# Two-layer hybrid decoder on eight cores: the last norm's gain and bias in one block on GpSimd, x loads and residual scaling moved into v_B and u

## The chip, the cores and the metric

The kernel runs on the 8 cores of one Trainium2 chip. Each core works alone on 8192 of the 65536 tokens (two sequences of 4096), with no communication between cores. The metric is the device time of the slowest core in microseconds (us). A core has TensorE for matmuls (PE in the profile; its weight loads are PEld), VectorE (DVE), ScalarE (ACT), GpSimd (POOL) and SyncE (SP), which issues DMAs here. Each engine works off its own instructions strictly in the order in which they were written; engines wait for each other through semaphores.

## The reference, cut to what matters

```python
x = _layernorm(x, ln_in_g, ln_in_b)
for l in range(2):
    h = x @ w_in[l] + b_in[l]
    q, k, v, g_a, u_b, v_b, g_b, r_a, r_b = _split_cols(h)
    y_a = _swa_sinks(q, k, v, sinks[l]) * silu(g_a)      # window 128, 8 query heads, 2 kv heads
    y_b = _chunked_sgu(gelu(u_b), gelu(v_b), ...) * silu(g_b)   # norm of v, 128x128 mixing per chunk
    merged = sigmoid(r_a) * (y_a @ p_a[l]) + sigmoid(r_b) * (y_b @ p_b[l])
    out = merged @ w_out[l] + b_out[l]
    x = _layernorm(ALPHA * x + out, ln_g[l], ln_b[l])
```

x is (16, 4096, 1024) in float32, D_MODEL is 1024, q, g_a, u_b, v_b and g_b are 512 columns wide, r_a and r_b 1024.

## The kernel before

**Tiles and stages.** Tokens go in tiles of 512 (four blocks j of 128 tokens). A stage is one tile in one layer; a core has 32 stages, numbered 0 to 31, ordered (tile 0, layer 0), (tile 1, layer 0), (tile 0, layer 1), (tile 1, layer 1), then tiles 2 and 3, and so on. So stages 4n and 4n+1 are layer 0 of a new pair of tiles, stages 4n+2 and 4n+3 are layer 1. **Kind 0, 1, 2 or 3** below is the stage number modulo 4. Stages 0 and 1, and 2 and 3, share some work; from stage 4 on all stages run the same loop.

**One stage of the loop, in PE's order.** First `out`: the output projection of the stage before, four blocks of 2x8 matmuls, reading the eight merged tiles `tRb` 0 to 7. Its first matmul is called the stage's *opening* here. Then `vb`, `u`, `gb`, `ga`: the projections v_B, u, gate_B, gate_A, four tiles of eight matmuls each; in `ga` each tile is followed by a spatial-gating step whose result VectorE turns into `mixed` and then into `gbT`. Then attention with the 16 tiles r of the two route projections: scores (`kpad,qT` in PE's rows) alternate with r tiles. Then `pb` (8 tiles, with transposes of the next stage's input), `q` of the next stage (4 tiles), `pa` (8 tiles) and `kv` of the next stage. In `pa` VectorE makes two instructions for each tile: `tRa<-tRa,ps` (from PSUM), then `tRb<-tRa,tRb`, an add whose inputs both lie in SBUF. The eighth add makes the last tile that `out` needs, in its eighth matmul.

**PSUM.** `q`, `kv`, `out`, `vb`, `u`, `gb`, `ga`, `pb` and `pa` rotate through five banks; r tiles have three and scores three. PE waits when the bank it needs has not been read out by ScalarE or VectorE.

**What sets the order.** The code is written region by region; *hooks* put extra steps behind a named tile: `("out", 2)` is behind block 2 of `out`, `("vb", 1)` behind the second v_B tile. A step joins each engine's queue there and is carried out when the queue comes to it, which may be long before PE reaches the named tile.

**The norm behind `out`.** VectorE adds the residual and takes statistics. After blocks 1 and 3 a variance goes to GpSimd, which raises it to the power -0.5 (`sm_p<-sm_p,neghalf`, `ln_rstd`); then VectorE forms the bias (`ln_bias`, L269 `sm_p<-mv_p,sm_p`) and ScalarE applies both (`second`, and `to_bf` when a layer follows). The gain and bias rows of the norm are applied by GpSimd two stages later in `third_hooks`: for each block four instructions `xres<-xres,gb` on 128x512 float32 (`ln_gb`), 16 in all, called *pieces* here. After layer 1 the block is then stored as y by SP. In kinds 0 and 1 the same buffer next takes the tile's new x (`load` in `resid_hooks`), which ScalarE scales (`app`, `xres<-xres,sm_i`) and GpSimd gives the input norm's gain and bias (again `ln_gb`, 16 pieces) as the residual.

**The input norm** of a new tile goes through `stg`: powers `sm_i` on GpSimd at ("q", 1) of kinds 2 and 3 and at ("vb", 1) of kinds 3 and 0; `lnin_hooks` puts the applications of blocks 2 and 3 (`xbf<-stg,sm_i`) behind u tiles.

**Weights** stream through four ring slots. SP loads them as bf16 from an internal buffer; at first use of each slab GpSimd issues the load from the float32 original (`ring<-wpk`), which happens up to stage 6.

Of the kernel before, what the change touches and what calls it, by code (L numbers as in the profile page):

```python
# [152 lines left out]
def build(n_tok, seq_len):  # L153
# [24 lines left out]
    def sb(name, shape, dt=F32):  # L178
        return es.enter_context(nc.sbuf_tensor(name, list(shape), dt))
# [24 lines left out]
    gb = sb("gb", [128, 6, D])  # L204
# [73 lines left out]
    def dma(eng, out, in_, reads, writes, chan, batch=False):  # L278
        P.add(eng, lambda e: e.dma_start(out=out, in_=in_), reads, writes, chan=chan, batch=batch)
# [86 lines left out]
    stages = []  # L366
# [108 lines left out]
    def ln_apply(k, j, out, okey, src, skey):  # L475
        j0 = j & ~1
        act(out, src, AF.Identity, (skey, ("sm1", k, j0), ("sm2", k, j0)), (okey,),
            bias=sm[k][:, 2, j:j + 1], scale=sm[k][:, 1, j:j + 1])

    def ln_gb(buf, j, gi, eng="pool"):  # L480
        key = ("xres", buf, j)
        for h in range(2):
            c = slice(h * 512, (h + 1) * 512)
            d = xres[:, buf, j, c]
            tt(eng, d, d, gb[:, gi, c], ALU.mult, (key, ("gb", gi)), (key,))
            tt(eng, d, d, gb[:, gi + 1, c], ALU.add, (key, ("gb", gi + 1)), (key,))
# [102 lines left out]
        for i, (k, f) in enumerate(zip(at[1:], (to_bf, second, to_bf, second))):  # L589
            hook(hooks, k, (lambda f, j: lambda: f(j))(f, 2 + i // 2))  # L590

    def third_hooks(s, hooks, at=(("out", 0), ("out", 1), ("out", 2), ("out", 3)),
                    to=(("vb", 0), ("vb", 1), ("vb", 2), ("u", 0))):

        t, l = stages[s]
        buf, gi = t % 2, 2 * (l + 1)

        def out_dma(j):
            r0 = t * 512 + j * 128
            dma("sp", y_d[r0:r0 + 128, :], xres[:, buf, j, :], (("xres", buf, j),), (("y", t, j),), ("yo", buf, j))  # L600
# [72 lines left out]
    def hook(hooks, k, f):  # L673
        hooks.setdefault(k, []).append(f)
# [38 lines left out]
    def lnin_hooks(s, hooks, at=(("vb", 1), ("u", 2), ("u", 3))):  # L713
        load, stats, apply = lnin_parts(s)
        hook(hooks, at[0], lambda: stats(2))
        hook(hooks, at[1], lambda: apply(2))
        hook(hooks, at[2], lambda: apply(3))

    def resid_hooks(s, hooks):
        t, l = stages[s]  # L720
        buf, k = t % 2, "i%d" % (t % 2)

        def load(j):
            r0 = t * 512 + j * 128
            dma("sp", xres[:, buf, j, :], x_d[r0:r0 + 128, :], (), (("xres", buf, j),), ("xr", buf, j))

        def app(j):
            d, key = xres[:, buf, j, :], ("xres", buf, j)
            ln_apply(k, j, d, key, d, key)

        if s < 2:
            at = (("r", 15), ("pb", 1), ("pb", 3), ("pb", 5))
        else:
            at = (("gb", 1), ("gb", 3), ("ga", 1), ("pb", 1))
        for j in range(4):
            if s > 1:
# [267 lines left out]
    for s in range(NS):  # L1004
        hooks = {}
# [23 lines left out]
        if s > 1:  # L1029
            third_hooks(s - 2, hooks, *THIRD.get(s, ()))  # L1030
        if s == NS - 1:
            third_hooks(s - 1, hooks, (("gb", 0), ("gb", 2), ("ga", 0), ("ga", 2)),
                        (("ga", 0), ("ga", 2), ("r", 0), ("r", 2)))
        if s == 3:
            lnin_hooks(s, hooks, (("r", 2), ("r", 6), ("r", 10)))
        elif s > 0 and is_lnin(s):
            lnin_hooks(s, hooks)
        if is_lnin(s + 1):
            lnin_before(s + 1, hooks)
        if stages[s][1] == 0:  # L1040
            resid_hooks(s, hooks)
# [94 lines left out]
```

How the kernel before makes its waits and increments, by code:

```python
        def run(ename, e):  # L100
            seen = {}
            for op in per_eng[ename]:
                waits = {}
                for d in op.deps:
                    if d.chan is None and d.eng == "pe" and ename == "pe" and op.chan is None:
                        continue
                    s, v = event(d)
                    if v > waits.get(s, (None, 0))[1]:
                        waits[s] = (s, v)
                if op.chan is not None and not self.chan_batch[op.chan] and op.ticket > 1:
                    s = csem[op.chan]
                    v = 16 * (op.ticket - 1)
                    if v > waits.get(s, (None, 0))[1]:
                        waits[s] = (s, v)
                for s, v in waits.values():
                    if seen.get(s, 0) < v:
                        e.wait_ge(s, v)
                        seen[s] = v
                ins = op.fn(e)
                if op.chan is not None:
                    ins.then_inc(csem[op.chan], 16)
                elif op.signal:
                    ins.then_inc(esem[ename], 1)
            if ename == "sp":
                for c, s in csem.items():
                    v = 16 * self.chan_count[c]
                    if seen.get(s, 0) < v:
                        e.wait_ge(s, v)
                        seen[s] = v
```

## Time and profile before

| | us |
|---|---|
| median of 3 runs | 3554.02 (3551.52 to 3555.46) |
| profiled execution | 3556.13 |
| its slowest core (core 2), span | 3554.5 |
| the other cores, span | 3531.3 to 3548.6 |
| PE busy | 3400.5 (96%) |
| DVE, ACT, POOL busy | 2316.1, 1814.9, 1396.1 |
| granted TensorE clock, core 2 | 0.989 |

All rows are of core 2. Times in the trace are counted from the start of the span. A matmul of 512 columns is shown with 0.38 us, but eight in a row take 1.89 us, so one starts every (1.89 - 0.38) / 7 = 0.216 us. In brackets behind a row stands how long the engine sat idle before it and what ended the wait. An instruction on VectorE or GpSimd that is itself held up shows as a longer one, not as idle time. Openings named below: stage 12 at 1383.00, stage 13 at 1493.22, stage 14 at 1600.28, stage 15 at 1706.70, stage 16 at 1812.29.

### The profile page before, as it was taken

How to read it: one execution, taken by the hardware profiler on the slowest of the kernel's cores; microseconds unless marked ns; L12 is line 12 of the kernel's file. 1: busy time of each engine (PE TensorE's matmuls, PEld its weight loads, DVE VectorE, ACT ScalarE, POOL GpSimd, SP SyncE). 2: the span in 40 equal slices, each digit the busy share in tenths (PEclk: the TensorE clock that was granted, in tenths of full speed). 3: DMA queues.
4: the chain of work that ended last, by engine and by line, in shares of the span. 5: the costliest groups of instructions: out<-in, count | busy, mean ns of one | idle time of the engine just before them, and what ended most of it. 6: DMA issues, size and time to landing. Idle time of an engine off the chain costs nothing.

```text
span 3554.5 us, 61689 instructions; the slowest of 8 cores (3531.3 to 3554.5 us)
## 1 busy us (share of the span) xinstructions
PE 3400.5 (96%) x18320; PEld 1596.8 (45%) x18320; DVE 2316.1 (65%) x4993; ACT 1814.9 (51%) x4059; POOL 1396.1 (39%) x1284
## 2 busy tenths in 40 slices
PE   5999889989999999999999999999999999999997
PEld 2444334434444444444444444444444444444443
DVE  3675665646766666766676666666667667666667
ACT  4455345635456445465445465455555554555543
POOL 1343243533245333452344432444134533255343
PEclk9999999999999999999999999999999999999999
DMA  9666875564444445354454444553445534455342
GB/s 183 157 163 115 223 177 184 172 178 160 160 165 171 163 149 186 136 174 146 168 194 152 147 147 161 197 184 130 149 149 190 184 137 156 154 170 192 137 137 108
DMA packets 97095, 577.77 MB, mean 163 GB/s; under 512 B 11010, under 2 KB 11266, under 8 KB 41348
## 3 DMA queue, kind: packets, MB, share of 16 engines
q1 hardware_dynamic: 90580, 535.08, 43.2%
q0 software_dynamic: 5472, 38.28, 6.9%
q8 instruction: 159, 2.61, 0.3%
q14 instruction: 164, 1.34, 0.1%
q10 hardware_dynamic: 720, 0.46, 0.1%
HBM read 550.18 MB, written 61.87 MB: 172 GB/s over the span
## 4 chain that ended last, share of the span: by engine, by line
PE 91%; DVE 3%; issue 2%; DMA 2%; ACT 2%; POOL 1%; DVEq 0%; SPq 0%; ACTq 0%; POOLq 0%
PE ps L248 88%; PE ps L495 2%; PE ps L894 2%; DMA ring<-wpk 1%; DVE gbT L259 1%; POOL xres L259 1%; DVE tRa L269 0%; DVE sm_i L269 0%; ACT xT L256 0%; ACT Pq L868 0%; ACT L868 0%; DVE nmx L861 0%; DMA xres<-x 0%; DVE ps L858 0%; DVE xres L269 0%
## 5 line engine op out<-in xcount | busy, mean ns | idle before, releaser
L248 PE MATMUL ps<-xT,ring 128*128 128x512 bf16 x8080 | 1875.1, 381 | 36.5 <-DMA ring<-wpk 30.0
L248 PEld LDWEIGHTS ps<-xT,ring 128*128 128x128 bf16 x8080 | 782.9, 98 | 965.5 <-issue 83.7
L259 POOL TENSOR_TENSOR xres<-xres,gb 128x512 f32<-128x512 f32 x762 | 987.5, 1300 | 206.9 <-ACT xres L256 124.5
L259 POOL TENSOR_TENSOR Pq<-Pq,rcp 128x512 bf16<-128x512 bf16 x256 | 261.4, 1042 | 1030.2 <-DVE rcp L881 836.3
L868 ACT ACTIVATE Pq<-ps,nmx 128x128 bf16<-128x128 f32 x1024 | 370.8, 374 | 314.1 <-DVE nmx L269 311.6
L248 PE MATMUL ps<-ring,tRb 128*128 128x512 bf16 x2016 | 443.6, 380 | 12.0 <-DMA ring<-wpk 9.7
L248 PEld LDWEIGHTS ps<-ring,tRb 128*128 128x128 bf16 x2016 | 196.3, 98 | 245.2 <-issue 20.0
L256 ACT ACTIVATE xres<-xres,sm_p 128x1024 f32<-128x1024 f32 (+1 forms) x129 | 155.6, 1218 | 273.5 <-DVE sm_p L269 270.5
L248 PE MATMUL ps<-ring,xT 128*128 128x128 bf16 (+1 forms) x1920 | 286.9, 300 | 0.0
L259 POOL TENSOR_TENSOR sm_p<-sm_p,neghalf 128x2 f32<-128x2 f32 (+1 forms) x66 | 45.7, 692 | 552.9 <-DVE sm_p L263 543.4
L248 PE MATMUL ps<-gbT,ring 128*128 128x512 bf16 x1024 | 256.0, 379 | 0.0
L861 DVE TENSOR_REDUCE nmx<-ps 128x2 f32<-128x256 f32 x512 | 217.5, 425 | 55.3 <-DVE ps L858 3.2
L269 DVE SCALAR_TENSOR_TENSOR tRa<-tRa,ps 128x512 bf16<-128x512 bf16 x256 | 174.1, 680 | 121.4 <-PE ps L248 121.2
L269 DVE SCALAR_TENSOR_TENSOR xres<-xres,ps 128x512 f32<-128x512 f32 x256 | 174.9, 683 | 89.6 <-PE ps L248 84.9
L248 PE MATMUL ps<-gaT,ring 128*128 128x512 bf16 x992 | 221.0, 379 | 6.5 <-DVE tRa L269 5.0
L248 PE MATMUL ps<-kpad,qT 128*128 128x512 bf16 x512 | 195.4, 382 | 32.5 <-DVE nmx L861 17.9
L256 ACT ACTIVATE xT<-ps,cs 128x512 bf16<-128x512 bf16 x256 | 185.7, 780 | 75.2 <-PE ps L495 75.1
L858 DVE COPY_PREDICATED ps<-upper,ps 128x256 f32<-128x256 uint16 x496 | 208.0, 419 | 12.2 <-PE ps L248 12.0
L868 ACT ACTIVATION_READ_ACCUMULATOR Pq<-ps,nmx 128x1 f32 x1024 | 214.9, 210 | 0.0
L259 DVE TENSOR_TENSOR uT<-uT,gbT 128x512 bf16<-128x512 bf16 x120 | 79.5, 673 | 202.5 <-ACT gbT L256 202.5
L256 ACT ACTIVATE xbf<-xres,sm_p 128x1024 bf16<-128x1024 f32 x64 | 79.1, 1236 | 251.3 <-DVE sm_p L269 251.3
L248 PEld LDWEIGHTS ps<-ring,xT 128*128 128x128 bf16 x1920 | 150.5, 98 | 121.5 <-issue 2.4
(117 smaller groups left out, 3773.2 us busy)
## 6 DMA issues: line engine op xcount, KB each, us to landing
ring<-ws SPq DMA_DIRECT2D x368, 1024.0 KB, 5.0
xres<-x SPq DMA_DIRECT2D x64, 512.0 KB, 8.1
y<-xres SPq DMA_DIRECT2D x60, 512.0 KB, 5.3
ring<-wpk POOLq DMA_DIRECT2D x29, 1024.0 KB, 13.5
stg<-x SPq DMA_DIRECT2D x56, 512.0 KB, 5.6
ws<-ring SPq DMA_DIRECT2D x25, 1024.0 KB, 10.8
ring<-ws SPq DMA_DIRECT2D x28, 512.0 KB, 3.7
gb<-gbr SPq DMA_DIRECT2D x6, 512.0 KB, 12.3
```

Of the source, the lines that this page charges most:

```text
L248: P.add("pe", lambda e: e.matmul(out, lhsT, rhs, start=start, stop=stop), reads, writes)
L256: P.add("act", lambda e: e.activation(out=out, in_=in_, func=func, **kw), reads, writes)
L259: P.add(eng, lambda e: e.tensor_tensor(out=out, in0=in0, in1=in1, op=op), reads, writes)
L269: P.add("dve", lambda e: e.scalar_tensor_tensor(out=out, in0=in0, scalar=s, in1=in1, op0=op0, op1=op1), reads, writes)
L495: P.add("pe", (lambda o, i: lambda e: e.transpose(out=o, in_=i, identity=ident_bf[:]))(o, i), (("xbf", j), ("ident",)), (("ps", BX),))
L858: P.add("dve", lambda e: e.copy_predicated(out=o[:, :, 1, :], mask=upper[:].bitcast(mybir.dt.uint16).rearrange("p (h k) -> p h k", h=2), d ...
L861: P.add("dve", lambda e: e.tensor_reduce(out=nmx[:, q, 2 * c:2 * c + 2], in_=o[:, :, 1, :], axis=mybir.AxisListType.X, op=ALU.max, negate= ...
L868: P.add("act", (lambda hk: lambda e: e.activation(out=Pq[:, q, hk * 4 + c, :], in_=o[:, hk, 1, :], func=AF.Exp, scale=0.125, bias=nmx[:, q ...
L894: P.add("pe", (lambda h: lambda e: e.transpose(out=psP[:, h * 128:(h + 1) * 128], in_=Pq[:, q, h, :], identity=ident_bf[:]))(h), (("Pq", q ...
```

## The change

```diff
-    def third_hooks(s, hooks, at=(("out", 0), ("out", 1), ("out", 2), ("out", 3)),
-                    to=(("vb", 0), ("vb", 1), ("vb", 2), ("u", 0))):
+    def third_hooks(s, hooks, at=(("out", 0),) * 4, to=(("out", 0), ("out", 1), ("out", 2), ("out", 3))):
...
         if s < 2:
             at = (("r", 15), ("pb", 1), ("pb", 3), ("pb", 5))
+        elif s % 2 == 0:
+            at = (("vb", 1), ("vb", 3), ("u", 1), ("u", 3))
         else:
-            at = (("gb", 1), ("gb", 3), ("ga", 1), ("pb", 1))
+            at = (("vb", 1), ("u", 0), ("u", 1), ("gb", 1))
         for j in range(4):
             if s > 1:
-                hook(hooks, (("u", 1), ("u", 2), ("u", 3), ("gb", 0))[j], (lambda j: lambda: load(j))(j))
+                hook(hooks, (("out", 3), ("vb", 0), ("vb", 1), ("vb", 2))[j], (lambda j: lambda: load(j))(j))
...
         elif s > 0 and is_lnin(s):
-            lnin_hooks(s, hooks)
+            if stages[s][1] == 0:
+                lnin_hooks(s, hooks, (("vb", 1), ("gb", 2), ("ga", 0)))
+            else:
+                lnin_hooks(s, hooks)
```

No instruction is added or removed. The default places of `third_hooks` are used from stage 4 on; stages 2 and 3, and the extra call in stage 31, name their own places and keep them. `resid_hooks` acts in kinds 0 and 1, the new `lnin_hooks` places in kind 0.

GpSimd's queue in a stage of kind 0, from the power at ("q", 1) of the stage before (`sm_i`) to the attention's scaling of probabilities (`Pq`). `sm_p` are the powers of the norm behind `out`, `sm_v` those of v_B, `xres` the pieces. Before:

```order
L259 TENSOR_TENSOR sm_i<-sm_i,neghalf 128x2
L273 COPY kpad<-kpad 128x2x128
L273 COPY vbuf<-vbuf 128x128
L259 TENSOR_TENSOR xres<-xres,gb 128x512 x4
L259 TENSOR_TENSOR sm_p<-sm_p,neghalf 128x2
L259 TENSOR_TENSOR xres<-xres,gb 128x512 x8
L259 TENSOR_TENSOR sm_p<-sm_p,neghalf 128x2
L259 TENSOR_TENSOR xres<-xres,gb 128x512 x4
L259 TENSOR_TENSOR sm_v<-sm_v,neghalf 128x2
L259 TENSOR_TENSOR sm_i<-sm_i,neghalf 128x2
L259 TENSOR_TENSOR sm_v<-sm_v,neghalf 128x2
L259 TENSOR_TENSOR xres<-xres,gb 128x512 x12
```

The same place in the changed kernel:

```order
L259 TENSOR_TENSOR sm_i<-sm_i,neghalf 128x2
L273 COPY kpad<-kpad 128x2x128
L273 COPY vbuf<-vbuf 128x128
L259 TENSOR_TENSOR xres<-xres,gb 128x512 x16
L259 TENSOR_TENSOR sm_p<-sm_p,neghalf 128x2 x2
L259 TENSOR_TENSOR sm_v<-sm_v,neghalf 128x2
L259 TENSOR_TENSOR sm_i<-sm_i,neghalf 128x2
L259 TENSOR_TENSOR xres<-xres,gb 128x512 x4
L259 TENSOR_TENSOR sm_v<-sm_v,neghalf 128x2
L259 TENSOR_TENSOR xres<-xres,gb 128x512 x12
```

The 16 pieces of the last norm stand together ahead of both `sm_p` powers, and the first four pieces of the residual stand between the two `sm_v` powers.

ScalarE's queue in a stage of kind 1, from the read-out of the v_B tiles (`vbg`) to the first gate_A tiles (`gaT`). `xres<-xres,sm_i` is the residual's scaling. Before:

```order
L256 ACTIVATE vbg<-ps 128x512 x4
L256 ACTIVATE xbf<-xres,sm_p 128x1024
L256 ACTIVATE uT<-ps,cs 128x512
L256 ACTIVATE xres<-xres,sm_p 128x1024
L256 ACTIVATE uT<-ps,cs 128x512 x2
L256 ACTIVATE xbf<-xres,sm_p 128x1024
L256 ACTIVATE uT<-ps,cs 128x512
L256 ACTIVATE gbT<-ps,cs 128x512
L256 ACTIVATE xres<-xres,sm_p 128x1024
L256 ACTIVATE gbT<-ps,cs 128x512
L256 ACTIVATE xres<-xres,sm_i 128x1024
L256 ACTIVATE gbT<-ps,cs 128x512 x2
```

In the changed kernel, over the middle of the same stretch:

```order
L256 ACTIVATE xres<-xres,sm_i 128x1024
L256 ACTIVATE xres<-xres,sm_p 128x1024
L256 ACTIVATE uT<-ps,cs 128x512
L256 ACTIVATE xres<-xres,sm_i 128x1024
L256 ACTIVATE uT<-ps,cs 128x512
L256 ACTIVATE xbf<-xres,sm_p 128x1024
L256 ACTIVATE uT<-ps,cs 128x512
L256 ACTIVATE gbT<-ps,cs 128x512
L256 ACTIVATE xres<-xres,sm_p 128x1024
L256 ACTIVATE gbT<-ps,cs 128x512
L256 ACTIVATE xres<-xres,sm_i 128x1024
L256 ACTIVATE gbT<-ps,cs 128x512 x2
```

Before, one of the four scalings stood ahead of the last two `gbT` read-outs; now all four do (the first, behind two of the `vbg` read-outs, is above the rows shown).

GpSimd's queue at the opening of stage 4, with the weight loads that GpSimd issues. Before:

```order
L273 COPY vbuf<-vbuf 128x128
L279 DMA ring<-wpk 128x4096
L259 TENSOR_TENSOR xres<-xres,gb 128x512 x4
L259 TENSOR_TENSOR sm_p<-sm_p,neghalf 128x2
L259 TENSOR_TENSOR xres<-xres,gb 128x512 x8
L259 TENSOR_TENSOR sm_p<-sm_p,neghalf 128x2
L259 TENSOR_TENSOR xres<-xres,gb 128x512 x4
L279 DMA ring<-wpk 128x4096 x2
```

In the changed kernel:

```order
L273 COPY vbuf<-vbuf 128x128
L279 DMA ring<-wpk 128x4096
L259 TENSOR_TENSOR xres<-xres,gb 128x512 x16
L259 TENSOR_TENSOR sm_p<-sm_p,neghalf 128x2 x2
L279 DMA ring<-wpk 128x4096 x2
```

Both powers now stand between the pieces and the two loads, of which the first fetches the gate_B slab.

## Rows read from the trace of the kernel before

**Rows 1.** The page, part 4: the chain that ended last, by engine

```profile
PE 91%; DVE 3%; issue 2%; DMA 2%; ACT 2%; POOL 1%; DVEq 0%; SPq 0%; ACTq 0%; POOLq 0%
```

**Rows 2.** Windows, stages 12 to 14: us; busy PE, PEld, DVE, ACT, POOL; clock; DMA

```profile
1383.00:1493.22 110.22, 106.85 (x575) 50.09 (x573) 73.85 (x158) 56.83 (x127) 53.92 (x47) 0.98 0.51 179
1493.22:1600.28 107.06, 105.36 (x576) 49.75 (x573) 71.64 (x147) 58.87 (x129) 53.02 (x46) 1.00 0.50 171
1600.28:1706.70 106.42, 105.48 (x576) 49.58 (x574) 70.43 (x153) 57.06 (x127) 32.34 (x31) 1.00 0.40 143
```

**Rows 3.** Timeline of PE, fourth scores of stages 12 and 13: start, us, what

```profile
1435.43 0.59 PE L248 MATMUL ps<-kpad,qT 128*128 128x512 bf16 x1 [3.24 <-DVE nmx L861]
...
1543.85 0.38 PE L248 MATMUL ps<-kpad,qT 128*128 128x512 bf16 x1 [1.44 <-ACT Pq L868]
```

**Rows 4.** Timeline of DVE, last gbT products of stages 12, 13, 14

```profile
1429.28 2.57 DVE L259 TENSOR_TENSOR gbT<-mixed,uT 128x512 bf16<-128x512 f32 x2
...
1537.77 2.51 DVE L259 TENSOR_TENSOR gbT<-mixed,uT 128x512 bf16<-128x512 f32 x2
...
1644.41 1.28 DVE L259 TENSOR_TENSOR gbT<-mixed,uT 128x512 bf16<-128x512 f32 x2
```

**Rows 5.** Timeline of POOL, stage 12

```profile
1372.00 5.50 POOL L259 TENSOR_TENSOR xres<-xres,gb 128x512 f32<-128x512 f32 x4
1392.99 0.70 POOL L259 TENSOR_TENSOR sm_p<-sm_p,neghalf 128x2 f32<-128x2 f32 x1 [15.49 <-DVE sm_p L263]
...
1421.94 17.89 POOL L259 TENSOR_TENSOR xres<-xres,gb 128x512 f32<-128x512 f32 x12 [9.19 <-ACT xres L256]
```

**Rows 6.** Timeline of DVE, `pa` ahead of stage 12's opening

```profile
1373.51 1.45 DVE L259 TENSOR_TENSOR tRb<-tRa,tRb 128x512 bf16<-128x512 bf16 x1
1374.88 0.67 DVE L269 SCALAR_TENSOR_TENSOR tRa<-tRa,ps 128x512 bf16<-128x512 bf16 x1
1375.66 0.71 DVE L259 TENSOR_TENSOR tRb<-tRa,tRb 128x512 bf16<-128x512 bf16 x1
...
1378.22 0.42 DVE L259 TENSOR_TENSOR tRb<-tRa,tRb 128x512 bf16<-128x512 bf16 x1
...
1383.85 0.42 DVE L259 TENSOR_TENSOR tRb<-tRa,tRb 128x512 bf16<-128x512 bf16 x1
```

**Rows 7.** Timeline of PE, kv tile and opening of stage 12

```profile
1379.49 1.89 PE L248 MATMUL ps<-xT,ring 128*128 128x512 bf16 x8 [0.21 <-DVE tRa L269]
...
1383.00 4.26 PE L248 MATMUL ps<-ring,tRb 128*128 128x512 bf16 x19
```

**Rows 8.** Timelines of POOL and DVE, `pa` ahead of stage 13's opening

```profile
1478.10 5.49 POOL L259 TENSOR_TENSOR xres<-xres,gb 128x512 f32<-128x512 f32 x4
...
1484.73 0.42 DVE L259 TENSOR_TENSOR tRb<-tRa,tRb 128x512 bf16<-128x512 bf16 x1
```

**Rows 9.** Timelines of DVE and ACT, stages 12 and 13

```profile
1406.36 0.21 DVE L263 TENSOR_SCALAR sm_i<-mv_i 128x2 f32<-128x2 f32 x1
...
1424.83 0.74 DVE L269 SCALAR_TENSOR_TENSOR mixed<-ps,cs,Cc 128x512 f32<-128x512 f32 x1
...
1518.41 1.24 ACT L256 ACTIVATE xbf<-xres,sm_p 128x1024 bf16<-128x1024 f32 x1 [2.75 <-DVE sm_p L269]
...
1532.07 1.48 DVE L269 SCALAR_TENSOR_TENSOR mixed<-ps,cs,Cc 128x512 f32<-128x512 f32 x2
```

**Rows 10.** Timelines of POOL and PE, stages 4 and 6

```profile
502.27 1.28 POOL L259 TENSOR_TENSOR xres<-xres,gb 128x512 f32<-128x512 f32 x1
...
525.51 1.15 POOL L279 DMA_DIRECT2D ring<-wpk  x2
...
539.20 3.15 PE L248 MATMUL ps<-xT,ring 128*128 128x512 bf16 x7 [17.96 <-DMA ring<-wpk]
...
729.18 5.51 POOL L259 TENSOR_TENSOR xres<-xres,gb 128x512 f32<-128x512 f32 x4
...
755.53 1.16 POOL L279 DMA_DIRECT2D ring<-wpk  x2
```

## The prediction

> **What bounds the kernel now.** I read the chain of waits first: 91% of it is PE [rows 1]. So a change pays only where PE stands still, and costs where it makes PE stand still. The windows from opening to opening then show how much there is to win [rows 2]: a stage of kind 2 takes 106.42 us, kind 1 107.06, kind 0 110.22 at a granted clock of 0.98; kind 3 is like kind 2 (its stage 15 lies between openings 1706.70 and 1812.29: 105.59). The excess of kinds 0 and 1 sits in one place: ahead of the fourth scores PE idles 3.24 us in stage 12 and 1.44 us in stage 13 [rows 3]. VectorE is late there. Its last two `gbT` products take 2.57 and 2.51 us in kinds 0 and 1 and 1.28 in kind 2 [rows 4], and only in kinds 0 and 1 does GpSimd work off residual pieces at that time (12 of them from 1421.94 on, 17.89 us, in stage 12) [rows 5].
>
> This is the mechanism on which everything below rests: a VectorE instruction with two SBUF inputs does not run beside a GpSimd piece. In [rows 5, 6] the four pieces start every (5.50 - 1.27) / 3 = 1.41 us (a single one takes 1.27) from 1372.00, so they end at 1373.27, 1374.68, 1376.09 and 1377.50. The two adds that fall among them end at 1374.96 and 1376.37, each 0.28 us behind the end of a piece, and take 1.45 and 0.71 us where a free one takes 0.42. The `tRa` product from PSUM keeps its 0.67. The Trainium skill has this as a rule (page SBUF — State Buffer, section Who interferes with whom): a VectorE instruction with two SBUF inputs and a GpSimd instruction that reads SBUF exclude each other for the whole instruction. The rows above agree as far as VectorE is concerned; GpSimd is a rival below.
>
> **Term 1: the last norm's 16 pieces, now behind the kv copies in one run.** Before, four of them ran there and the others behind the powers. They wait for nothing, so they start where the first four start now, and cover `pa`.
>
> Kinds 0 and 3, worked on stage 12. Pieces now go on ending at 1378.91, 1380.32, 1381.73, 1383.14, 1384.55, 1385.96. The third add, ready at 1378.22, ends at 1378.91 + 0.28 = 1379.19. The next product starts 0.08 before an add ends (1374.88 against 1374.96 [rows 6]), and its add is ready 0.78 later, before the next piece ends: the adds now follow at 1.41 us instead of 1.13. The eighth ends at 1379.19 + 5 x 1.41 = 1386.24; before it ended at 1383.85 + 0.42 = 1384.27 [rows 6]. Two things wait. The kv tile already waits for the bank of the fourth product [rows 7]; that product starts at 1379.11 instead of 1378.56, so kv and the opening move by 0.55, to 1383.55. The eighth matmul of `out`, 7 x 0.216 = 1.51 later at 1385.06, needs the eighth add; with the 0.2 us that PE takes to follow VectorE it starts at 1386.44: another 1.38. Together **1.93 us** for each of the 12 stages 7, 8, 11, 12, ..., 27, 28: 23.2 us.
>
> Kind 1, worked on stage 13: the pieces start at 1478.10, one ends at 1485.01; the first add (ready 1484.73 [rows 8]) ends at 1485.29, the eighth 7 x 1.41 = 9.87 later at 1495.16. The eighth matmul of `out` would start at 1493.22 + 1.51 = 1494.73 and now starts at 1495.36: **0.63 us**, for 7 stages of kind 1 and for stage 31, which has no `sm_i` power ahead of it: 5.0 us. Kind 2 starts its pieces some 7 us earlier, since the residual pieces at ("pb", 1) are gone and nothing holds the copies; the run ends at about the opening and spares the last add. By its phase that costs 0.1 to 1.1; I take 0.3, near the lower end, because the first add is then ready just as a piece ends. Six stages: 1.8 us. Term 1 is **+30.0 us**; the bounds are 20 (half of the kind 0 and 3 price, if adds slip into the 0.14 us between pieces) and 40.
>
> What this run does not cost, from stage 7 on: the `sm_p` power. The pieces end at 1372.00 + 15 x 1.41 + 1.27 = 1394.4; the power's input is there at 1393.0 [rows 5]. It comes some 1.4 us late, and VectorE asks for it only behind the statistics of block 2, which it takes another 3 us to reach. Five banks stand behind that.
>
> **Term 2: residual scaling and pieces in vb and u.** The intention is that GpSimd is done before the `gbT` products. I find that it is not. Kind 0: the first four pieces stand behind the `sm_i` power, whose variance VectorE has only at 1406.36 + 0.21, 23.6 us after the opening [rows 9]; powers and pieces then run without a gap: 24.2 + 16 x 1.41 + 0.7 = 47.5 us after the opening, 48 with the stretching by the `gbT` products. VectorE, on time, is through with `gbT` and takes up the scores at 45.4 (in kind 2: 1644.41 + 1.28 - 1600.28 [rows 4]). GpSimd is therefore busy at the place where the 3.24 us are lost, and now also through u and gb, where the normalised v, the `uT` products and the input norm's bias (which `lnin_hooks` now puts behind the third of them, with ScalarE's application behind it) each wait for the end of a piece. VectorE reaches the first `mixed` of `ga` about 41.7 us after the opening, as now (1424.83 - 1383.00 [rows 9]). What is won is the part of the scores behind 48 us: I take **-0.5 us**, x 6 (stages 8 to 28) = -3.0. If VectorE were on time, kind 0 would win 110.22 - 106.42 less the rest that kind 2 does not have: up to 4.8.
>
> Kind 1 has no `sm_i` power, but ScalarE has three more scalings of 1.24 us ahead of the last `gbT` read-outs (order rows of the change), 3.7 us. Its wait of 2.75 us for the `sm_p` bias [rows 9] shrinks to about 1, since that power no longer stands behind pieces: the read-outs come about 2 us later. Pieces run from 23.6 to about 47 us after the opening. With the `uT` products waiting for them, the first `mixed` starts 41.1 us after the opening instead of 1532.07 - 1493.22 = 38.85 [rows 9]. From there to the end of the last `gbT` stage 12 takes 7.0 us: 48.1 instead of 47.1 (1537.77 + 2.51 = 1540.28 [rows 4]). So I expect **+1.1 us** here, x 7 = 7.7; the bounds are -1.55 (no wait left at the scores) and +2.2. Term 2 is **+4.7 us**, from -40 to +20.
>
> **Term 3: stages 4 and 6, where GpSimd also issues weight loads.** In stage 4 a load holds the pieces back until 502.27 [rows 10]. They now end at 502.27 + 22.6 = 524.9, the first power at 525.6. Only then can VectorE go on to block 3 (two residual adds, statistics, variance: 3.7 us), and the second power ends at 530.0. Behind it stand the gate_B and gate_A loads: issued at 530.6 instead of 525.51. PE waits for the gate_B load (17.96 us until 539.20 [rows 10]), so that moves by **+5.1 us**. PE runs out of banks meanwhile, but the remaining tile of vb and the four of u take 9 us, at half clock 18, and fit before 544. Stage 6: 729.18 + 22.4 = 751.6, power 752.3, block 3 to 755.8, power 756.5, loads at 757.0 instead of 755.53 [rows 10]: **+1.5 us**. Term 3 is +6.6, up to 12 if stage 4's scalings wait for x behind the weight traffic.
>
> **y stores and x loads** go ahead of the weight loads in SP's queue. The fourth store waits for the last piece, about 11.4 us after the opening; the next weight loads wait for the end of `out`, 13.9 us after it, anyway. The x loads are out by 15 us and land before the scalings need them. Price 0; if x came late, ScalarE would stand at ("vb", 1) with five banks of slack.
>
> **Sum.** 30.0 + 4.7 + 6.6 = 41.3 us. The profiled execution took 3556.1 with a span of 3554.5 and the median is 3554.0; I take the sum as a difference to the median: 3595.3.
>
> **The rivals.**
> *A, the scores are freed after all.* VectorE and ScalarE catch up because some waits overlap. Kind 0 wins 3.4 (left with what kind 1 loses now), kind 1 1.55: 6 x 3.4 + 7 x 1.55 = 31.3 instead of a loss of 4.7: 3554.0 + 30.0 - 31.3 + 6.6 = 3559.3. For it speaks that every residual piece starts over 10 us earlier than now; against it the count of 1.41 us slots above.
> *B, faster.* As A, and also the whole 4.8 in kind 0 (8.4 more), and VectorE's adds in `pa` lose only half (15 less): 3559.3 - 8.4 - 15 = 3535.9. It decides at the eighth add: if that ends less than 1.5 us behind the opening, the run is free. Against it stand the two adds among pieces, which show exactly the slot.
> *C, the scores get worse.* If in both kinds `gbT` ends 1.5 us later still, PE idles past 3.2 us in kind 1 too, and the clock falls as it does in stage 12 (0.98 in its window): about 2.4 us more in 13 stages: 3626.
> *D, the exclusion also holds GpSimd.* Pieces and adds would then alternate at 1.27 + 0.42 + 0.14 = 1.83 us, not 1.41: about 2.5 us more per stage of kinds 0 and 3, 3 of the others, 3665. Four pieces take 5.50 us with adds among them and 5.49 without [rows 5, 8], which speaks against it. The Trainium skill (same page and section) has the loser fully blocked, whichever engine it is, and so gives D; the rows bear out only half of it.
> *E, the change does not do what it says.* The order rows show that it does.
>
> **How the numbers follow.** Forecast 0.55, with a range of its own from 3578 to 3612; A 0.17; B 0.08; C 0.17; D 0.03. A measurement of this kernel can tell about 0.2%, 7.1 us, from no change, so "same" is 3546.9 to 3561.1. B is faster (0.08); of A some 0.11 lies within; the rest, 0.81, is slower. The range leaves out B, D, the lower part of A and the upper part of C: 3557 to 3620.
>
> **What would show it.** Right: in `pa` all eight adds about 1.41 us apart; PE idle at 1.5 us behind the openings of kinds 0 and 3, released by VectorE's `tRb`; GpSimd still in `xres` pieces at the first scores of kinds 0 and 1; stage 4's gate_B load some 5 us later. Wrong: adds at 1.13 us, or GpSimd idle when the third `gbT` product starts.

## The result: 1.5% slower, and the profile after

| | before | after |
|---|---|---|
| profiled execution, us | 3556.1 | 3607.5 (another run: 3606.3) |
| slowest core, span, us | 3554.5 | 3605.9 |
| ratio of the runs | | 1.015 (1.012 to 1.018) |
| granted clock, slowest core | 0.989 | 0.984 |

So about 53 us were lost, where 41.3 were forecast. Two other executions of the changed kernel were disturbed and are left out.

The page of after, part 4 (the chain by engine, beside [rows 1]) and from part 5 the adds of `pa` and the matmuls of `out`; the last row is the same group of adds before, from the view by lines:

```profile
PE 88%; DVE 5%; issue 2%; DMA 2%; POOL 2%; ACT 1%; DVEq 0%; SPq 0%; POOLq 0%; ACTq 0%
...
L248 PE MATMUL ps<-ring,tRb 128*128 128x512 bf16 x2016 | 451.1, 381 | 29.4 <-DVE tRb L259 20.0
...
L259 DVE TENSOR_TENSOR tRb<-tRa,tRb 128x512 bf16<-128x512 bf16 x256 | 180.6, 705 | 26.7
```

```profile
L259 DVE TENSOR_TENSOR tRb<-tRa,tRb 128x512 bf16<-128x512 bf16 x256 | 130.4, 509 | 26.7
```

An add of `pa` now takes 705 ns in the mean, before 509, and `out` waits 20.0 us for them. The windows of after (openings: stage 12 at 1400.70, 13 at 1512.40, 14 at 1622.30, 15 at 1729.80, 16 at 1837.20; columns as in [rows 2]):

```profile
1400.70:1512.40 111.70, 107.29 (x576) 50.19 (x573) 79.30 (x157) 56.91 (x127) 57.76 (x50) 0.98 0.51 170
1512.40:1622.30 109.90, 107.21 (x577) 50.02 (x575) 73.84 (x147) 59.01 (x130) 60.30 (x52) 0.98 0.47 169
1622.30:1729.80 107.50, 105.60 (x575) 49.54 (x573) 69.93 (x156) 57.10 (x127) 22.75 (x24) 1.00 0.42 145
1729.80:1837.20 107.40, 105.66 (x576) 49.60 (x574) 73.15 (x165) 55.14 (x126) 32.96 (x31) 1.00 0.44 153
```

Beside [rows 2] the stage of kind 0 lost 1.5 us, that of kind 1 2.8 us (and its granted clock went from 1.00 to 0.98), that of kind 2 1.1 and that of kind 3 1.8. Summed over all openings of the slowest cores: kind 1 20.1 us (7 stages), kind 0 9.5 (6, stages 8 to 28), kind 3 10.6 (6, stages 7 to 27), kind 2 5.8 (6, from stage 10), stage 4 2.6, stage 6 0.6, stage 31 0.4, and 1.6 up to stage 4's opening, which no edit explains: 51.2 of the 51.4 between the spans.

**In `pa`.** GpSimd and VectorE ahead of stage 12's opening, and PE there. Of VectorE four of the eight adds are shown and the small `sm_i` bias step, which is held like an add (1.22 us):

```profile
1389.35 22.07 POOL L259 TENSOR_TENSOR xres<-xres,gb 128x512 f32<-128x512 f32 x16
...
1390.85 1.45 DVE L259 TENSOR_TENSOR tRb<-tRa,tRb 128x512 bf16<-128x512 bf16 x1
...
1393.64 1.22 DVE L269 SCALAR_TENSOR_TENSOR sm_i<-mv_i,sm_i 128x2 f32<-128x2 f32 x1
...
1398.46 0.71 DVE L259 TENSOR_TENSOR tRb<-tRa,tRb 128x512 bf16<-128x512 bf16 x1
...
1399.88 0.71 DVE L259 TENSOR_TENSOR tRb<-tRa,tRb 128x512 bf16<-128x512 bf16 x1
...
1402.70 0.70 DVE L259 TENSOR_TENSOR tRb<-tRa,tRb 128x512 bf16<-128x512 bf16 x1
```

```profile
1397.20 1.89 PE L248 MATMUL ps<-xT,ring 128*128 128x512 bf16 x8 [0.57 <-DVE tRa L269]
...
1400.71 1.81 PE L248 MATMUL ps<-ring,tRb 128*128 128x512 bf16 x7
1403.55 2.75 PE L248 MATMUL ps<-ring,tRb 128*128 128x512 bf16 x12 [1.03 <-DVE tRb L259]
```

The adds end 1.41 us apart, and the eighth at 1403.40, 2.69 us behind the opening. PE waits for it: two matmuls start 1.19 us further apart than the usual 0.216, and with the delay of the matmul before them PE loses 1.33 us.

**At the scores.** PE at the fourth scores of stages 12 and 13 and the r tile behind those of 13 (as [rows 3]); VectorE's last `gbT` products (as [rows 4]); GpSimd in stage 12:

```profile
1454.58 0.38 PE L248 MATMUL ps<-kpad,qT 128*128 128x512 bf16 x1 [3.29 <-DVE nmx L269]
...
1564.47 0.58 PE L248 MATMUL ps<-kpad,qT 128*128 128x512 bf16 x1 [2.43 <-ACT Pq L869]
1565.05 3.27 PE L248 MATMUL ps<-xT,ring 128*128 128x512 bf16 x8
```

```profile
1448.43 2.57 DVE L259 TENSOR_TENSOR gbT<-mixed,uT 128x512 bf16<-128x512 f32 x2
...
1558.49 2.52 DVE L259 TENSOR_TENSOR gbT<-mixed,uT 128x512 bf16<-128x512 f32 x2
```

```profile
1432.61 17.84 POOL L259 TENSOR_TENSOR xres<-xres,gb 128x512 f32<-128x512 f32 x12
```

In kind 1 `gbT` ends 48.6 us behind the opening (1561.01 - 1512.40) instead of 47.1. PE's idle time grew by 1.0 us, from 1.44 to 2.43, and now the clock falls: the eight matmuls behind it start every (3.27 - 0.38) / 7 = 0.41 us instead of 0.216, which is another 7 x 0.197 = 1.4 us. In kind 0 the idle time is the same as before, 3.29 us against 3.24, and the clock falls as before. GpSimd's last piece ends at 1450.45, 49.7 us behind stage 12's opening: it is still busy at `gbT`, as forecast.

### The profile page after: what moved, and what is told of

It is laid out like the page before. It is cut to its first block, busy times and chain, and to the rows that moved or that the text cites. A ratio compares the mean times of both kernels' runs of the same rounds, so it can differ in the third digit from the quotient of the medians.

```text
span 3605.9 us, 61689 instructions; the slowest of 8 cores (3579.7 to 3605.9 us)
## 1 busy us (share of the span) xinstructions
PE 3425.7 (95%) x18320; PEld 1601.7 (44%) x18320; DVE 2367.7 (66%) x4993; ACT 1817.1 (50%) x4059; POOL 1408.7 (39%) x1284
## 3 DMA queue, kind: packets, MB, share of 16 engines
q14 instruction: 164, 1.34, 0.1%
## 4 chain that ended last, share of the span: by engine, by line
PE 88%; DVE 5%; issue 2%; DMA 2%; POOL 2%; ACT 1%; DVEq 0%; SPq 0%; POOLq 0%; ACTq 0%
PE ps L248 84%; PE ps L495 2%; PE ps L895 2%; DVE tRa L269 1%; POOL xres L259 1%; DMA ring<-wpk 1%; DVE gbT L259 1%; DVE tRb L259 1%; DVE nmx L862 0%; DVE sm_i L269 0%; DVE ps L859 0%; DMA ws<-ring 0%; ACT xT L256 0%; DMA xres<-x 0%; DVE xres L269 0%
## 5 line engine op out<-in xcount | busy, mean ns | idle before, releaser
L248 PE MATMUL ps<-xT,ring 128*128 128x512 bf16 x8080 | 1887.2, 383 | 22.0 <-DMA ring<-wpk 10.6
L248 PE MATMUL ps<-ring,tRb 128*128 128x512 bf16 x2016 | 451.1, 381 | 29.4 <-DVE tRb L259 20.0
L259 DVE TENSOR_TENSOR uT<-uT,gbT 128x512 bf16<-128x512 bf16 x120 | 91.7, 776 | 182.7 <-ACT gbT L256 182.3
L259 DVE TENSOR_TENSOR tRb<-tRa,tRb 128x512 bf16<-128x512 bf16 x256 | 180.6, 705 | 26.7
```

The lines of the kernel that those rows point to most:

```text
L248: P.add("pe", lambda e: e.matmul(out, lhsT, rhs, start=start, stop=stop), reads, writes)
L259: P.add(eng, lambda e: e.tensor_tensor(out=out, in0=in0, in1=in1, op=op), reads, writes)
```

## The experiments

### Each part alone

The pieces alone (`e1_third_only`, an edit of the kernel before), and the residual alone (`e2_resid_only`, an edit of the changed kernel):

```diff
-    def third_hooks(s, hooks, at=(("out", 0), ("out", 1), ("out", 2), ("out", 3)),
+    def third_hooks(s, hooks, at=(("out", 0),) * 4,
```

> The kernel before with one part of the change: all 16 pieces of the last norm at ("out", 0); y stores, x loads and residual scaling stay where they were. My theory (terms 1 and 3 of the prediction, re-read from the trace of after: openings of kinds 0 and 3 stand 1.36 us longer, x 12; 0.43 x 7 and 0.83 x 6 in kinds 1 and 2; the kv tile 0.3 x 18; stages 4 and 6 3.2) gives 16.3 + 3.0 + 5.0 + 5.4 + 3.2 = 32.9 us, so 3587; by the prediction's own numbers 36.6, 3591. Rival: GpSimd is idle through v_B instead, the powers and the u products come earlier and the fourth scores of kinds 0 and 1 with them: 1.4 to 3.4 us back in 13 stages, 3555 to 3570.

```diff
-    def third_hooks(s, hooks, at=(("out", 0),) * 4, to=(("out", 0), ("out", 1), ("out", 2), ("out", 3))):
+    def third_hooks(s, hooks, at=(("out", 0), ("out", 1), ("out", 2), ("out", 3)),
+                    to=(("out", 0), ("out", 1), ("out", 2), ("out", 3))):
```

> The changed kernel with the 16 pieces of the last norm back at ("out", 0) to ("out", 3): the residual's part alone (y stores, x loads, scalings, bias of the input norm). My theory: the parts add up. The trace of after puts 2.9 us x 7 on kind 1 (fourth scores stand 3.7 instead of 1.8 us and the clock falls behind them) and nothing net on kind 0: +20 us, 3574, adds in pa at 0.42 us again but for the first ones. The prediction's term 2 gives +4.7, 3559. Rival: the parts need each other; with 12 pieces of the last norm still in v_B, the residual's pieces queue behind them, end 5 us later still, and the scores of kinds 0 and 1 wait longer than in the full change: 3590 or more.

Measured for the pieces: 1.0038 (1.0023 to 1.0054), some 13 us. That lies in the range of the rival (3555 to 3570), not at the theory's 3587. The waits of the theory are all there: 1.3 us at the openings of kinds 0 and 3, 0.4 at those of kind 1 and 1.3 at those of kind 2 (0.6 in stage 18), and some 0.35 us more at the kv tiles ahead of the openings of kinds 0 and 3, 30 us in all. But kind 0 became 2.0 us *shorter* than before, as the rival had it. The window of its stage 12 (opening 1390.10), then from its timelines PE at the fourth scores, ScalarE's application of the input norm and GpSimd's first power of v_B, and last the same application and the same power in the kernel before:

```profile
1390.10:1498.30 108.20, 105.55 (x575) 49.64 (x573) 73.69 (x157) 56.94 (x127) 57.59 (x50) 1.00 0.50 178
```

```profile
1441.88 0.38 PE L248 MATMUL ps<-kpad,qT 128*128 128x512 bf16 x1 [1.29 <-ACT Pq L868]
...
1419.40 1.24 ACT L256 ACTIVATE xbf<-stg,sm_i 128x1024 bf16<-128x1024 f32 x1 [0.29 <-DVE sm_i L269]
...
1411.70 0.69 POOL L259 TENSOR_TENSOR sm_v<-sm_v,neghalf 128x2 f32<-128x2 f32 x1 [2.71 <-DVE sm_v L263]
```

```profile
1414.03 1.24 ACT L256 ACTIVATE xbf<-stg,sm_i 128x1024 bf16<-128x1024 f32 x1 [3.31 <-DVE sm_i L269]
...
1405.28 5.51 POOL L259 TENSOR_TENSOR xres<-xres,gb 128x512 f32<-128x512 f32 x4
1410.74 0.70 POOL L259 TENSOR_TENSOR sm_v<-sm_v,neghalf 128x2 f32<-128x2 f32 x1
```

Before, the powers of v_B and of the input norm stood behind pieces on GpSimd (the first `sm_v` power starts 27.7 us behind the opening, right behind four pieces), and ScalarE waited 3.31 us for the bias that comes of them. With the pieces alone moved, the block ends 10.7 us behind the opening and that power starts at 21.6, as soon as its input is there. ScalarE waits 0.29 us, all `gbT` read-outs come 1.7 us earlier (33.6 instead of 35.3 us behind the opening), PE idles 1.29 instead of 3.24 us and the clock stays up. Beside the 1.3 us that its opening now costs, a stage of kind 0 has therefore won 3.3 us, and one of kind 1 0.5: 23 us that the prediction did not have. VectorE's small steps there are also free of pieces (0.16 instead of 0.60 us for the `sm_p` bias); no run tells their share from that of the powers.

Measured for the residual: 1.053 (1.048 to 1.058), some 180 us. The theory (3574) is far off. The rival (3590 or more) has the side, but neither the size nor the place: the stages of kinds 0 and 1 take 119 to 125 us. SP, ScalarE and PE in stage 12 of this kernel (opening 1426.5):

```profile
1442.78 11.90 SPq L279 DMA_DIRECT2D y<-xres  x3
1454.83 0.34 SPq L279 DMA_DIRECT2D xres<-x  x1
...
1459.69 1.24 ACT L256 ACTIVATE xres<-xres,sm_i 128x1024 f32<-128x1024 f32 x1 [14.67 <-DMA xres<-x]
...
1461.56 8.71 PE L248 MATMUL ps<-xT,ring 128*128 128x512 bf16 x26 [8.16 <-ACT vbg L256]
```

The y stores wait for pieces that end at 1454.3; the first x load stands behind them in SP's queue and goes out 28 us behind the opening, where "by 15" was forecast; ScalarE stands at the first scaling with two `vbg` read-outs behind it, and PE runs out of banks. So the two parts are not independent: the residual's move costs this little only because the pieces are done 11 us behind the opening.

### Which piece costs what in the changed kernel

Kind 1 back at its old places (`e3_kind1_back`):

```diff
-            at = (("vb", 1), ("u", 0), ("u", 1), ("gb", 1))
+            at = (("gb", 1), ("gb", 3), ("ga", 1), ("pb", 1))
```

(and its x loads at u 1 to gb 0).

> The changed kernel, with x loads and residual scalings and pieces of kind 1 (stages 5, 9, ..., 29) back at their old places. My theory: the 2.9 us that each stage of kind 1 lost come from the residual's earlier pieces and scalings in that stage: 7 x 2.9 = 20 us back, 3586; PE idle at the fourth scores of kind 1 falls from 2.6 to about 1.4 us and the matmuls behind it run at 0.216 us again. Rival: kind 1 is late because of what the stage before and the pieces of the last norm left (its opening's wait, the powers): under 5 us back, 3601 to 3606.

Measured 1.0085 (1.0067 to 1.0103), 3584: 22 us back, the first theory. Kind 1 takes 106.9 us again at full clock. Then the residual's pieces left out (`e4_no_resid_pieces`) and the last norm's (`e5_no_last_norm_pieces`):

```diff
-            hook(hooks, at[j], (lambda j: lambda: (app(j), ln_gb(buf, j, 0)))(j))
+            hook(hooks, at[j], (lambda j: lambda: (app(j), ln_gb(buf, j, 0) if s < 2 else None))(j))
```

> The changed kernel without the 16 pieces of the residual in kinds 0 and 1 (the input norm's gain and bias are left out of the residual there, 14 stages; scalings, loads and stores stay). Theory P, VectorE is late at the fourth scores because of GpSimd's pieces: the wait falls to the 0.25 us of kind 2, the clock stays up: 3.4 + 1.7 + 0.4 = 5.5 us x 6 of kind 0 and 3.4 + 0.7 + 0.4 = 4.5 us x 7 of kind 1, 64 us: 3542. Theory S, the scalings on ScalarE ahead of the last gbT read-outs make it: they stay, and so does most of the wait: 3595 or more.

```diff
-            hook(hooks, at[j], (lambda j: lambda: ln_gb(buf, j, gi))(j))
+            if s < 2 or s == NS - 2:
+                hook(hooks, at[j], (lambda j: lambda: ln_gb(buf, j, gi))(j))
```

> The changed kernel without the 16 pieces of the last norm in stages 4 to 31 (that norm's gain and bias are left out there; stage 31's extra block stays). What the block costs in all in the changed kernel. My theory of the slots: openings without a wait (1.34 x 6, 0.43 x 6, 0.89 x 6, 1.39 x 6) and the kv tile without its 1.2 us in kinds 2 and 3: 24 + 14 = 38 us; the gate_B loads of stages 4 and 6 no longer behind pieces: 15 to 24 us. 3606 - 53 to 62 = 3544 to 3553, and the scores of kinds 0 and 1 as in the changed kernel (3.7 us). Rival: the waits at the openings come from other steps of VectorE; they stay in part, and the gain is under 25 us plus the loads: 3560 or more.

Without the residual's pieces: 0.9967 (0.9951 to 0.9983), 3542, which is theory P. The scalings are all there, and the waits at the scores are gone. Its stages 12 and 13, and its last `gbT` products:

```profile
1379.70:1486.20 106.50, 104.69 (x562) 49.70 (x573) 69.12 (x157) 56.82 (x127) 35.96 (x34) 1.00 0.51 180
1486.20:1592.20 106.00, 104.69 (x561) 49.56 (x572) 66.24 (x147) 58.88 (x129) 38.59 (x36) 1.00 0.51 178
```

```profile
1424.93 1.28 DVE L259 TENSOR_TENSOR gbT<-mixed,uT 128x512 bf16<-128x512 f32 x2
```

Without the last norm's: 0.9986 (0.9967 to 1.0004), some 3549. The slowest cores of the profiled executions (3542.2 and 3605.9) lie 64 us apart. By stages it is 40 at the openings and kv tiles (38 forecast) and 24.5 in stages 4 and 6 (15 to 24 forecast). Its stages 14 and 15 show what kinds 2 and 3 are without a piece near `pa`; even the four pieces of the kernel before cost them some 0.9 us:

```profile
1587.00:1692.60 105.60, 104.39 (x562) 49.74 (x573) 66.75 (x155) 57.06 (x127) 12.40 (x15) 1.00 0.44 152
1692.60:1797.80 105.20, 104.40 (x561) 49.73 (x572) 69.71 (x163) 55.08 (x125) 12.43 (x14) 1.00 0.44 148
```

### Better places

The price of a piece depends on what VectorE does beside it. Four kernels try other places, all edits of the kernel before. `w1_resid_in_r`:

```diff
-            at = (("gb", 1), ("gb", 3), ("ga", 1), ("pb", 1))
+            at = (("r", 3), ("r", 7), ("r", 11), ("pb", 1))
```

> The kernel before with one edit: from stage 4 on the residual's scalings and pieces at ("r", 3), ("r", 7), ("r", 11) and ("pb", 1), each block right behind a pair of probability scalings (Pq) of GpSimd. My theory (VectorE is late at the fourth scores only because of GpSimd's pieces in gb and ga, as the run without them showed): kinds 0 and 1 come to 106.4 and 105.8 us, so 6 x 3.8 + 7 x 1.1 = 31 us are won: 3523. Between two Pq pairs GpSimd stands idle 7 us, four pieces take 5.5. Rival: inside attention the pieces hold VectorE's small row-maximum steps (1.2 instead of 0.16 us) and through them ScalarE's exponentials, and PE waits for scores or for Pq: more than 2.4 us per stage lost again, 3554 or more.

`w2_block0_pb`: that, and in stages 5 to 30

```diff
+            third_hooks(s - 1, hooks, (("pb", 2),), (("q", 3),), blocks=(0,))
```

with blocks 1 to 3 left at out 1 to 3 of the next stage.

> As the kernel with the residual in attention, and the pieces of block 0 of the last norm at ("pb", 2) of the stage before, so that pa has no pieces from stage 6 on. My theory of the slots: adds in pa take 0.42 us throughout, the kv tile's wait of 0.9 to 1.0 us in kinds 2 and 3 falls to about 0.5: 12 x 0.4 = 5 us below that kernel, 3518. Rival: eight pieces behind the last Pq (11.3 us) hold GpSimd's sm_i power and the copies of kpad and vbuf ahead of kv and cost PE more than that: 3525 or more.

`w3_r_gaps` and `w4_stage4`:

```diff
+        R4 = (("r", 3), ("r", 7), ("r", 11), ("pb", 1))
...
+        elif s % 4 == 2:
+            third_hooks(s - 2, hooks, R4)
...
+        if s > 6 and s % 4 == 3 and s < NS - 1:
+            third_hooks(s - 1, hooks, R4, (("r", 7), ("r", 11), ("r", 15), ("pb", 5)))
```

> As the kernel with block 0 in pb, and moreover the 16 pieces of kinds 2 (from stage 6) and those of kind 0 (one stage earlier, in kind 3, with their y stores) between the Pq pairs too; only stages of kind 1 and 3 keep 12 pieces in out and v_B. Theory: what a piece costs is where it meets VectorE's two-input SBUF instructions; out and v_B of kinds 0 and 2 are free then, which gives ScalarE 1.7 us there, of no use where PE does not wait. Stage 6's gate_B load on GpSimd no longer stands behind 16 pieces: up to 12 us (the wait of 12.15 in stage 6). 3507 to 3515. Rival: y stores behind pieces in SP's queue hold weight loads, as they did with the residual's part alone: PE waits for a DMA in kind 3, 3530 or more.

```diff
+        if s == 4:
+            third_hooks(2, hooks, (("u", 2), ("gb", 0), ("gb", 2), ("ga", 0)), tuple(("r", i) for i in range(4)))
```

(and stage 4's residual: loads at r 4 to 7, scalings and pieces at r 11, r 15, pb 2, pb 5).

> As the kernel before it, and in stage 4 the last norm's pieces behind u and gb tiles, the residual's x loads and pieces in attention: the gate_B load on GpSimd stands behind no piece. Theory: the load goes out up to 20 us earlier and PE's 18 us wait for it goes: 12 to 18 us below that kernel, 3490 to 3500. Rival: the load waits for its ring slot or the memory, not for GpSimd's queue: under 4 us.

Measured, in this order: 0.998 (0.997 to 0.9991); 0.995 (0.993 to 0.997); 1.005 (1.003 to 1.007); 1.001 (1.000 to 1.002). In us these are some 3544, 3532, 3568 and 3554, where 3523, 3518, 3507 to 3515 and 3490 to 3500 were expected: all four came out slower than their theories, though the second lies 13 us below the first where 5 were expected. The last two also apply a gain and bias to three blocks of tile 1's residual in stage 1 (12 more pieces), a slip of the stage numbers that costs 4.7 us in that stage. What else was missed lies in the stages with pieces in attention, which is a bad place for them: kinds 0 and 1 take 108.0 us with three blocks in it, so kind 0 wins 2.3 and kind 1 loses 1.1. Kinds 2 and 3 take 105.2 to 105.6 us in the second kernel, with nothing in `pa`, and 108.5 to 108.9 in the third, with pieces in attention. VectorE and ScalarE in stage 12 of the first kernel: a row-maximum step is held (0.66 us), and the exponential waits for it.

```profile
1450.12 0.66 DVE L269 SCALAR_TENSOR_TENSOR nmx<-nmx,nsink 128x2 f32<-128x2 f32 x1
...
1450.87 0.37 ACT L868 ACTIVATE Pq<-ps,nmx 128x128 bf16<-128x128 f32 x1 [1.22 <-DVE nmx L269]
```

Between the last two lie some 14 us, as forecast (12 to 18): stage 4's last two loads on GpSimd went out at 510.31 instead of 525.42 (525.51 in the kernel before [rows 10]).

The next kernels follow from that: pieces behind `pb`, where VectorE works from PSUM, none in `pa`, and in attention from stage 7 on none but block 2 of the residual in the second. `w5_combined`, `w6_combined_r3` (with `at = (("gb", 1), ("gb", 3), ("r", 3), ("pb", 1))` for the residual) and `w7_final`, whose core is

```diff
+        O2 = (("out", 0), ("out", 0), ("out", 1), ("out", 2))
...
+        elif s == 6:
+            third_hooks(4, hooks, (("gb", 1), ("gb", 3), ("ga", 1), ("pb", 1)))
+        elif s > 7 and s % 4 in (0, 3):
+            third_hooks(s - 2, hooks, O2, blocks=(2, 3))
+        elif s > 6:
+            third_hooks(s - 2, hooks, blocks=(1, 2, 3))
...
+        if 5 < s < NS - 1:
+            third_hooks(s - 1, hooks, (("pb", 2), ("pb", 4)), (("q", 3), ("pa", 0)),
+                        blocks=(0, 1) if s > 6 and s % 4 in (2, 3) else (0,))
```

> The kernel before with the last norm's pieces where neither pa nor attention has any: from stage 7 on blocks 0 and 1 (kinds 3 and 0) or block 0 (kinds 1 and 2) behind pb tiles 2 and 4 of the stage before, the rest behind out 1 and 2; in stage 4 behind u and gb with the residual in attention, in stage 6 in attention. The residual stays in gb and ga. My theory, from stage lengths measured so far: kinds 2 and 3 105.2 us (1.0 less each, x 12), kind 0 about 107 to 108 (8 instead of 12 pieces in out and v_B: up to the 1.7 us at ScalarE's gbT read-outs that the block gave, and the clock's fall behind the fourth scores), kind 1 106.9; stages 4 and 6 24 us less: 3554 - 12 - 15 - 24 = 3503. Rival: pieces behind pb hold the sm_i power and the copies ahead of kv, and PE loses there what it wins in pa: 3520 or more.

> As the combined kernel, and in kinds 0 and 1 block 2 of the residual at ("r", 3) instead of ("ga", 1): 8 pieces instead of 12 ahead of the fourth scores, 4 between the first two Pq pairs. Theory: the gbT products lose their waits (fourth scores as in kind 2), 1.5 us in kind 1 and 1.5 to 2.5 in kind 0, while one block in attention costs a third of the 2.4 us that three cost: about 1 us less per stage x 13 against the combined kernel, 3490. Rival: the first 8 pieces start so late (gb 1) that they still cover gbT; then nothing is won and the block in attention costs 0.8 x 13 = 10 us: 3513.

> The combined kernel, with stage 6's 16 pieces at the places that the residual's pieces have in kinds 0 and 1 (gb 1, gb 3, ga 1, pb 1) instead of between the Pq pairs, and one block of the last norm in stage 6's pb. Theory: stage 6 falls from 109.8 to about 107 us, the rest is as in the combined kernel (kinds 0 to 3 at 107.0, 106.9, 105.2, 105.3 us): 3492 to 3496, a ratio of 0.983. Rival: what the combined kernel won was one good run (its interval reached to 0.995): 3510 or more.

Measured for `w5_combined`: 0.988 (0.981 to 0.995), with 3494.7 and 3525.2 us, where 3503 was expected. For `w6_combined_r3` there are 3502.0 and 3506.0 us and no ratio; 3490 was expected, and kind 1 takes 107.3 instead of 107.0. For `w7_final`: **0.986 (0.983 to 0.988)** where 0.983 was expected. That is 51 us faster than the kernel before and, by the two ratios, some 104 faster than the change. Stages 12 to 15 of w7 and an add of its `pa` (opening 1336.10), on core 0 with a span of 3485.3; the slowest core, 7, took 3505.7 at a granted clock of 0.988, and 107.8 and 108.1 us in kinds 0 and 1:

```profile
1336.10:1443.30 107.20, 105.35 (x577) 49.78 (x575) 71.80 (x155) 56.95 (x128) 48.90 (x43) 1.00 0.51 177
1443.30:1550.20 106.90, 105.30 (x576) 49.71 (x574) 71.51 (x147) 58.87 (x129) 53.02 (x46) 1.00 0.48 168
1550.20:1655.80 105.60, 105.21 (x576) 49.74 (x574) 69.16 (x155) 57.06 (x127) 37.37 (x35) 1.00 0.42 148
1655.80:1761.00 105.20, 105.16 (x575) 49.69 (x573) 70.09 (x163) 55.13 (x125) 32.61 (x30) 1.00 0.48 164
```

```profile
1327.63 0.42 DVE L259 TENSOR_TENSOR tRb<-tRa,tRb 128x512 bf16<-128x512 bf16 x1
```

## Why the prediction was right, and where it was right for the wrong sizes

The time (3607 against 3595.3) lies in the range and on the forecast side. The parts did less well than the sum, and that the sum came so close is partly luck: a gain of 23 us was not foreseen, and beside it term 2 cost 42 us where 4.7 stood, past its bound of 20. These two misses have opposite signs.

- **Term 1, the slots: right.** The adds follow at 1.41 us, and the eighth ends 2.69 us behind the opening (forecast 1386.24 - 1383.55 = 2.69). PE waits 1.3 to 1.4 us at the openings of kinds 0 and 3 (1.38 forecast), some 0.35 at the kv tile ahead of them (0.55), 0.43 in kind 1 (0.63) and 0.3 to 0.9 in kind 2 (0.3). That is 28 us in all, and 30 with the pieces alone, against 30.0: kind 2 was sized too small, the kv tile and kind 1 too large.
- **What the block gives: missed.** "What this run does not cost" looked at the `sm_p` power only. The other powers and the bias of the input norm got free of pieces, which is worth 3.3 us per stage of kind 0 and 23 us in all. The block alone, without stages 4 and 6, costs 6 to 10 us and not 30.
- **Term 2: right place, wrong size.** Its -0.5 for kind 0 is nearly what before and after show between them: 1.6 more per stage, of which 1.34 are the opening. But that near zero is a gain of 3.3 from the block and a loss of 3.6 by the residual's pieces, behind which the same bias is late again: ScalarE waits 3.84 us for it in stage 12 (row below). For kind 1 the end of `gbT` was well placed (48.6 against 48.1), 1.55 us later where I took 1.1. What failed is the next step, that PE pays only the delay: behind an idle time of 2.43 us the clock fell, which the prediction had kept for rival C "past 3.2 us". Kind 1 lost 2.5 us beside its opening's 0.43 (1.0 of idle time and 1.4 of clock in stage 13), 17 us in 7 stages instead of 7.7. Against the kernel with the pieces alone term 2 is +42 us.

```profile
1441.06 1.24 ACT L256 ACTIVATE xbf<-stg,sm_i 128x1024 bf16<-128x1024 f32 x1 [3.84 <-DVE sm_i L269]
```

- **Term 3: right in kind, half the size.** Stage 4 +2.6, stage 6 +0.6, where 5.1 and 1.5 stood. Stage 4's load went out at 527.72 (forecast 530.6), since its pieces began at 500.70, not 502.27. PE now idles 14.70 us ahead of the last vb tile, behind the late power, and 5.94 for the load: 20.6 in all, against 17.96 for the load alone before. The load stood behind the pieces already before, and that was the larger matter: without the last norm's pieces the two stages are 24.5 us shorter than in the changed kernel.

```profile
524.30 0.58 PE L248 MATMUL ps<-vbb,row 128*128 128x512 bf16 x1 [14.70 <-DVE xres L269]
...
542.17 11.31 PE L248 MATMUL ps<-xT,ring 128*128 128x512 bf16 x40 [5.94 <-DMA ring<-wpk]
```

- **y and x traffic at 0: right, and only together.** Its premise, the fourth store at 11.4 us, is what the residual alone does not have; there it cost 180 us. The five banks named as slack cover 6.5 of the 14.67 us that ScalarE then stands.
- **Rivals.** A was half true: the scores are freed by the block, and taken again by the residual. B fell with the eighth add. C's mechanism came true in kind 1, at a shorter idle time. In kind 0 the clock had fallen before too, but for stage 8, and stage 8 lost 2.9 us where the other stages of kind 0 lost 1.0 to 1.7. D: the 16 pieces take 22.07 us with eight adds among them, (22.07 - 1.27) / 15 = 1.39 us each, so the adds did not hold GpSimd. The Trainium skill (page SBUF — State Buffer, section Who interferes with whom) lets either engine be the blocked one, and for these adds the trace bears out one direction only.

## What to carry to other kernels

Price a helper engine's block twice: by what it meets where it goes, and by what was queued behind it where it was; the second can be the larger, and here it took a run of each part alone to show both. Parts of a change may need each other (here a store's premise was another part's early end), so the sum of parts measured apart is no estimate of the whole. Small waits ahead of TensorE are not paid one to one: one more microsecond of idle time in kind 1 cost 2.5, since the clock fell with it.

## What was not expected of the hardware

- **A one-input step waits too.** Among pieces, `vnh` (a TENSOR_SCALAR with one tensor input) takes 2.82 us for two where two free ones take 1.00. In after, stage 12, and with the pieces alone:

```profile
1432.75 2.82 DVE L265 TENSOR_SCALAR vnh<-vbg,mv_v,sm_v 128x512 bf16<-128x512 f32 x2 [1.90 <-POOL sm_v L259]
```

```profile
1418.18 1.00 DVE L265 TENSOR_SCALAR vnh<-vbg,mv_v,sm_v 128x512 bf16<-128x512 f32 x2 [0.20 <-POOL sm_v L259]
```

  The mechanism of the prediction ("two SBUF inputs") was too narrow. The Trainium skill (same page and section) names `tensor_scalar` among the operations that can contend, in a two-port mode. The trace agrees as to the wait and does not show the mode. VectorE's statistics of v_B beside pieces kept 0.68 us (at 1427.48 in stage 12 of after).
- **GpSimd is held by some products.** 12 pieces beside `uT` and `gbT` products took 17.84 us, (17.84 - 1.27) / 11 = 1.51 each, against 1.39 beside the adds of `pa`. Over the whole trace of after, pieces beside a `gbT` product (float32 `mixed` and bf16 `uT`) start 1.68 us apart in the median, those beside a `uT` product (bf16 throughout) 1.41.
- **The clock.** It fell to its lower level (1.2 instead of 2.4 GHz: matmuls 0.41 instead of 0.216 us apart) behind idle times of 2.43 and 3.29 us at the fourth scores, and did not behind 1.29 and 1.57 (the last in stage 9 of w7, core 0). But the length of that one wait does not decide it. In stage 8 of the kernel before PE idles 3.28 us and goes on at 0.216 us, and in stage 29 of w7, core 0, the matmuls behind 1.75 us start (3.01 - 0.38) / 7 = 0.38 us apart. The rows of the two stages of w7, then stage 8 of the kernel before:

```profile
1069.34 0.38 PE L248 MATMUL ps<-kpad,qT 128*128 128x512 bf16 x1 [1.57 <-ACT Pq L872]
1069.91 1.89 PE L248 MATMUL ps<-xT,ring 128*128 128x512 bf16 x8 [0.20 <-ACT tRa L256]
...
3192.48 0.38 PE L248 MATMUL ps<-kpad,qT 128*128 128x512 bf16 x1 [1.75 <-ACT Pq L872]
3192.96 3.01 PE L248 MATMUL ps<-xT,ring 128*128 128x512 bf16 x8
```

```profile
1007.18 0.38 PE L248 MATMUL ps<-kpad,qT 128*128 128x512 bf16 x1 [3.28 <-ACT Pq L868]
1007.65 1.89 PE L248 MATMUL ps<-xT,ring 128*128 128x512 bf16 x8
```

  What else decides it no run here shows. A price for a wait of 1.7 to 3.3 us is therefore a range, with and without the fall of the clock.
